# Reordering one-hots, gate copies and gate sums between the operand splits of a gate tile

## The chip, the cores and the metric

One core of one Trainium2 chip. The metric is the device time of one execution in microseconds; the kernel before took 3062.44 us (median of 3 runs, 3058.03 to 3063.49).

## The reference, cut to what matters

Two transformer blocks run over 256 tokens of width 2048 in float32. The first has an attention mixer and then a mixture over 16,384 tiny experts (`peer`); the second is another hybrid block. The change lies in `peer`:

```python
q = (xt @ wq).reshape(T, PEER_HEADS, 2, PEER_QDIM // 2)
...
idx = e1 * PEER_NKEYS + e2                  # 8 heads x 16 experts per token
gate = jax.nn.softmax(sc, axis=-1)
...
h = jax.nn.gelu(jnp.einsum('cd,chkd->chk', xc, u[ic]))
return jnp.einsum('chk,chkd->cd', gc * h, v[ic])
```

The kernel doesn't gather. It computes the hidden value of every expert for every token, builds a dense table of gates (zero where an expert wasn't chosen), multiplies the two and mixes all rows of `v`.

## The kernel before, in words

**Weights and splits.** All weights stream through two raw buffers of 1 MB (`raw`, 128 x 2048 floats); SyncE (SP) loads one such tile after another. A tile has two halves of 1024 columns. Each half is split into two reduced-precision parts that TensorE (PE) multiplies: ScalarE (ACT) writes `high` (`split_high`, L2270, the instruction is L2275), VectorE (DVE) writes `low = raw - high` (`split_low`, L1292, instruction L1296). There are four high and four low buffers. Half h uses buffer h % 4, and `split_high` waits until PE has used half h - 4 (`half_used`) and until the raw tile has landed. SP loads a raw buffer again when the low of its second half is written (`load`, L555). DVE and ACT work three halves ahead of PE (`LOOKAHEAD`).

**Experts, first pass.** 128 tiles of `u`, in 32 quads of four. For each tile, PE's `expert_hidden` (L1117) does, for either half, eight matmuls of 512 columns (high x both parts of the activations) and eight of 256 columns (low x high part). Every second tile, ACT copies the first results of a pair of tiles to SBUF (`first_hidden`, L2487, instruction L2493), DVE adds the second ones (`sum_hidden`, L1683, L1687), ACT applies gelu one tile later (`gelu`, L2496, L2499), and SP stores the pair, 256 KB, to `hidden_dram` (`store_hidden`, L574), in its queue between two loads.

**Gate tiles.** In quads 12 to 27 (16 quads, 64 tiles) each expert tile carries beside this the gates of four tokens. DVE's `onehots` (L1805) makes three tiles of 128x512: `first` (L1810), `second` (L1812), and `first_low` (L1815, `first` times the low part of the gate). ACT's `gate_first` (L2513, L2520) writes `first_high`, `first` times the high part of the gate, four instructions of 128x128. PE's `gates` (L1135) multiplies the one-hots of the four tokens after the tile's `expert_hidden`: four matmuls of 256 columns into two of the banks 4 to 7. There are two slots (`SLOTS`) for one-hots and for the result. Then ACT copies the high half of the result to `gates_out` (`copy_gates`, L2524, L2528) and DVE adds the low half (`sum_gates`, L1842, L1847). After each quarter (16 tiles, 64 tokens) ACT's queue issues eight stores of 512 KB to `gates_dram` (`store_gates`, L2547), one per tile in the first eight tiles of the next quarter; the last eight follow in the tiles behind the stage.

**The order of the work** is written out by hand for each engine; every engine takes its instructions in that order. In gate tile j of a quad both DVE and ACT split halves 2j + 3 and 2j + 4 and make the one-hots of tile j + 1:

- ACT: hidden step (`first_hidden` in even tiles, `gelu` in odd ones), two highs, `gate_first` of j + 1, `copy_gates` of j, and in some tiles a gate store.
- DVE: in even tiles `sum_hidden`, then two lows, `onehots` of j + 1, `sum_gates` of j.
- PE: `expert_hidden` of j (a wait for low in each half, one for the sum two tiles back), then `gates` of j, which waits for the sum of two tiles before (`gates_copied`), for the one-hots and for `first_high`.

Behind the stage come 16 expert tiles without gates, then the second pass over `v`.

Of the kernel before, what the change touches and what calls it, by code (L numbers as in the profile page):

```python
# [35 lines left out]
T = 256  # L36
# [7 lines left out]
LOOKAHEAD = 3  # L44
# [23 lines left out]
GATE_PIECES = 8  # L68
QUARTER = 64
# [14 lines left out]
CHOICE_QUADS = 12  # L84
PICK_ROWS = 4
GATE_QUADS = 16
# [21 lines left out]
def build(nc, ins, out):  # L108
    ctx = ExitStack()
    with ctx:  # L110
# [146 lines left out]
        def gate_parts(c):  # L257
            return bank[:, 4 + 2 * c:6 + 2 * c, :].rearrange("p b (u s e) -> p s e (b u)", s=2, e=P)
# [18 lines left out]
        dt_w = r4.take(KT * SSM_HEADS, "p (k n) -> p k n", k=KT)  # L277
        causal = r4.take(T)
        logits2, probs_t2, _, negmax2, expsum2 = attention_buffers(r4)
        dt_ = r4.take(4 * TT * SSM_HEADS, "p (k n) -> p k n", k=4)  # L280
        dt_tmp = r4.take(3 * TT * SSM_HEADS, "p (k n) -> p k n", k=3)
# [180 lines left out]
        def half(name, p, quad=0):  # L462


            q, p = quad + (quads[name] + p // QUAD), p % QUAD
            return p % SPLIT, p // 2 % RAW, p % 2, 2 * q + p // 4
# [58 lines left out]
        for n in range(UNITS):  # L525
            double, j, g = n // (2 * SET), n % (2 * SET) // 2, n % 2
# [4 lines left out]
                q=q1[part_of, c + (8 if swa else 0), :], k=k1[part_of, branch, :],  # L531
# [738 lines left out]
        def _(dve):  # L1270
# [21 lines left out]
            def split_low(h):  # L1292

                b, r, which, used = h
                dve.wait_ge(high_ready[b], used + 1)
                dve.tensor_tensor(low[b][:, :], raw[r][:, HALF * which:HALF * (which + 1)], as_f32(high[b][:, :]),  # L1296
                                  ALU.subtract).then_inc(low_ready[b], 1)
# [385 lines left out]
            def sum_hidden(n, j):  # L1683

                at = hidden[:, j % 2, :].rearrange("p (e t) -> p e t", e=2)
                dve.wait_ge(hidden_first, 2 * n + (j + 1))
                dve.tensor_tensor(at, at, bank[:, 2 * (j % 2):2 * (j % 2) + 2, T:], ALU.add).then_inc(hidden_summed, 1)  # L1687
# [111 lines left out]
            def split_tile_low(name, n, j):  # L1799
                if j % 2 == 0:  # L1800
                    sum_hidden(n, j // 2 - 1)
                split_low(half(name, 2 * j + LOOKAHEAD, n))
                split_low(half(name, 2 * j + LOOKAHEAD + 1, n))

            def onehots(n, j):  # L1805

                n, j = (n + 1, 0) if j == 4 else (n, j)
                c, token = j % SLOTS, 4 * FOUR * n + FOUR * j
                dve.wait_ge(gates_done[c], 2 * n + (j // 2 + PRIMED))
                dve.tensor_tensor(first[:, c, :, :], row(picked_t[:, 0, bass.ds(token, FOUR)], P), copies(iota[:, :], FOUR),  # L1810
                                  ALU.is_equal).then_inc(first_ready[c], 1)
                dve.tensor_tensor(second[:, c, :, :], row(picked_t[:, 1, bass.ds(token, FOUR)], P), copies(iota[:, :], FOUR),  # L1812
                                  ALU.is_equal)
                dve.wait_ge(first_ready[c], 2 * n + (j // 2 + 1))
                dve.tensor_tensor(first_low[:, c, :, :], first[:, c, :, :], row(picked_low[:, bass.ds(token, FOUR)], P), ALU.mult  # L1815
                                  ).then_inc(onehots_ready[c], 1)
# [25 lines left out]
            def sum_gates(q, n, j):  # L1842

                c = j % SLOTS
                at = gates_out[:, q % 2, :, bass.ds(4 * FOUR * n + (FOUR * j - QUARTER * q), FOUR)]
                dve.wait_ge(gates_first[c], 2 * n + (j // 2 + 1))
                dve.tensor_tensor(at, at, gate_parts(c)[:, 1], ALU.add).then_inc(gates_copied[c], 1)  # L1847

            def gate_tile(q, n, j, last=False):

                split_tile_low("experts_u_t", n + CHOICE_QUADS, j)
                if not last:
                    onehots(n, j + 1)
                sum_gates(q, n, j)

            onehots(0, 0)
            for q in range(T // QUARTER):
                with dve.Fori(GATE_QUADS // 4 * q, GATE_QUADS // 4 * (q + 1) - (q == T // QUARTER - 1)) as n:
                    for j in range(4):
                        gate_tile(q, n, j)  # L1860
            for j in range(4):
                gate_tile(T // QUARTER - 1, GATE_QUADS - 1, j, last=j == 3)
            with dve.Fori(0, EXPERT_QUADS - CHOICE_QUADS - GATE_QUADS - 1) as n:
                for j in range(4):
                    split_tile_low("experts_u_t", n + (CHOICE_QUADS + GATE_QUADS), j)
# [274 lines left out]
            for g in range(11):  # L2140
# [14 lines left out]
                for k in range(2):  # L2155
                    c, n = 4 * g + 2 * k, N * ((g - 3) % 2)
# [107 lines left out]
        def _(act):  # L2264
# [5 lines left out]
            def split_high(h):  # L2270

                b, r, which, used = h
                act.wait_ge(raw_landed[r], 16 * used + 16)
                act.wait_ge(half_used[b], used + PRIMED)
                act.activation(high[b][:, :], raw[r][:, HALF * which:HALF * (which + 1)], ACT.Copy  # L2275
                               ).then_inc(high_ready[b], 1)
# [210 lines left out]
            def first_hidden(n, j):  # L2487

                b, _, _, used = half("experts_u_t", 4 * j + 3, n)
                act.wait_ge(half_used[b], used + 1 + PRIMED)  # L2490
                if not (isinstance(n, int) and n == 0):
                    act.wait_ge(hidden_stored[j], 16 * n)
                act.activation(hidden[:, j, :].rearrange("p (e t) -> p e t", e=2), bank[:, 2 * j:2 * j + 2, 0:T],  # L2493
                               ACT.Copy).then_inc(hidden_first, 1)

            def gelu(n, j):  # L2496

                act.wait_ge(hidden_summed, 2 * n + (j + 1 + PRIMED))
                act.activation(hidden[:, j, :], hidden[:, j, :], ACT.Gelu_apprx_tanh).then_inc(gelu_done, 1)  # L2499

            def split_tile_high(name, n, j):
                split_high(half(name, 2 * j + LOOKAHEAD, n))
                split_high(half(name, 2 * j + LOOKAHEAD + 1, n))

            def hidden_tile(n, j):

                if j % 2 == 0:
                    first_hidden(n + (j // 2 - 1), 1 - j // 2)
                elif not (isinstance(n, int) and n == 0 and j == 1):
                    gelu(n + (j // 2 - 1), 1 - j // 2)  # L2510
                split_tile_high("experts_u_t", n, j)

            def gate_first(n, j):  # L2513

                n, j = (n + 1, 0) if j == 4 else (n, j)
                c = j % SLOTS
                act.wait_ge(first_ready[c], 2 * n + (j // 2 + 1))
                act.wait_ge(gates_done[c], 2 * n + (j // 2 + PRIMED))
                for t in range(FOUR):
                    m = act.activation(first_high[:, c, t, :], first[:, c, t, :], ACT.Copy,  # L2520
                                       scale=picked_t[:, 2, bass.ds(4 * FOUR * n + (FOUR * j + t), 1)])
                m.then_inc(first_high_ready[c], 1)

            def copy_gates(q, n, j):  # L2524

                c = j % SLOTS
                act.wait_ge(gates_done[c], 2 * n + (j // 2 + 1 + PRIMED))
                act.activation(gates_out[:, q % 2, :, bass.ds(4 * FOUR * n + (FOUR * j - QUARTER * q), FOUR)],  # L2528
                               gate_parts(c)[:, 0], ACT.Copy).then_inc(gates_first[c], 1)
# [22 lines left out]
                at = slice(piece * EXPERT_TILES // GATE_PIECES, (piece + 1) * EXPERT_TILES // GATE_PIECES)  # L2552
                act.dma_start(gates_dram[q, :, at, :], gates_out[:, q % 2, at, :]).then_inc(gates_stored[q % 2], 16)

            def gate_tiles(q, n, store=False, last=False):
                for j in range(4):
                    hidden_tile(n + CHOICE_QUADS, j)
                    if not (last and j == 3):
                        gate_first(n, j + 1)
                    copy_gates(q, n, j)  # L2560
                    if q and store:
                        store_gates(q - 1, 4 * (n - GATE_QUADS // 4 * q) + j)

            gate_first(0, 0)
            for q in range(T // QUARTER):
                if q >= 2:
                    act.wait_ge(gates_stored[q % 2], 16 * GATE_PIECES * (q // 2))
                for n in range(GATE_QUADS // 4 * q, GATE_QUADS // 4 * q + GATE_PIECES // 4):
                    gate_tiles(q, n, store=True)
                with act.Fori(GATE_QUADS // 4 * q + GATE_PIECES // 4, GATE_QUADS // 4 * (q + 1) - (q == T // QUARTER - 1)) as n:  # L2570
                    gate_tiles(q, n)
            gate_tiles(T // QUARTER - 1, GATE_QUADS - 1, last=True)
            for n in range(CHOICE_QUADS + GATE_QUADS, CHOICE_QUADS + GATE_QUADS + GATE_PIECES // 4):
                for j in range(4):
                    hidden_tile(n, j)
# [346 lines left out]
```

## Time and profile before

| | |
|---|---|
| median of 3 runs | 3062.44 us |
| the profiled execution | 3059.4 us, of which span 3057.6 |
| PE, DVE, ACT busy in the span | 3019.4, 2028.6, 1538.2 us |
| TensorE clock granted | 0.999 of full over the span |
| HBM traffic | 578.13 MB read, 36.49 MB written |

All durations below come from that one execution; times of day are microseconds from the start of its span. "Busy" counts the bars of an engine's instructions. Matmuls are pipelined and the end of a bar is modelled, so bars of neighbouring matmuls overlap. A merged row of the timeline (x8) gives the start of the first instruction and the time to the end of the last. `[0.67 <-ACT high L2275]` is idle time ahead of a row and what ended it.

### The profile page before, as it was taken

Reading aid. Unit: us, or ns where it says so; the run is one execution under the profiler, and the core shown is the slowest. Engines: PE = TensorE matmul, PEld = TensorE weight load, DVE = VectorE, ACT = ScalarE, POOL = GpSimd, SP = SyncE. Lnnn points to the kernel's source line nnn. Section 1 sums busy time; section 2 is a strip of 40 time slices with the busy share of each in tenths; the row PEclk is TensorE's granted clock in tenths of the full one; section 3 lists DMA queues with packets and bytes.
Section 4 is the critical chain, followed back from the end, with each engine's and each line's share of the span. In section 5 each row is a group of like instructions: output and inputs, shape, how many; then the busy total and the mean of one; then the engine's idle time right before and its main releaser. Section 6 shows DMA issues by size and latency. Waiting matters only on the chain.

```text
span 3057.6 us, 45171 instructions
## 1 busy us (share of the span) xinstructions
PE 3019.4 (99%) x16816; PEld 2615.9 (86%) x16816; DVE 2028.6 (66%) x2694; ACT 1538.2 (50%) x2134; POOL 20.6 (1%) x42
## 2 busy tenths in 40 slices
PE   9998999999999999999999999999999999999999
PEld 8997898888888888888888888888889888888887
DVE  5566679976888875555555555776566777777443
ACT  4554534555666665444444444544555555555333
POOL 2000000000000000000000000000000000000000
PEclk9999999999999999999999999999999999999999
DMA  7333545565566568766666666444455555555554
GB/s 269 133 132 116 188 159 196 204 228 187 186 239 240 213 219 296 249 240 242 242 241 241 241 241 233 163 147 163 152 179 179 181 195 187 191 180 192 196 189 179
DMA packets 138979, 615.20 MB, mean 201 GB/s; under 512 B 12989, under 2 KB 50062, under 8 KB 73968
## 3 DMA queue, kind: packets, MB, share of 16 engines
q1 hardware_dynamic: 126976, 583.05, 54.0%
q10 hardware_dynamic: 9440, 21.93, 2.0%
q0 software_dynamic: 2464, 8.89, 0.9%
q8 instruction: 63, 1.03, 0.1%
q14 instruction: 36, 0.29, 0.0%
HBM read 578.13 MB, written 36.49 MB: 201 GB/s over the span
## 4 chain that ended last, share of the span: by engine, by line
PE 76%; ACT 6%; DVE 5%; issue 3%; DMA 3%; ACTq 0%; DVEq 0%; SPq 0%
PE bank L642 75%; DMA raw<-in_experts_u_t 3%; ACT high L2275 3%; DVE low L1296 3%; ACT first_both L2520 1%; DVE first L1810 1%; ACT big L2528 1%; ACT big L2499 0%; ACT big L2493 0%; PE bank L912 0%; PE bank L732 0%; DMA raw<-in_w_down_t 0%; DVE resid L1928 0%; DVE big L1722 0%; ACT big L2307 0%
## 5 line engine op out<-in xcount | busy, mean ns | idle before, releaser
L1296 DVE TENSOR_TENSOR low<-raw,high 128x1024 fp32r<-128x1024 f32 x1008 | 1225.4, 1223 | 823.4 <-ACT high L2275 819.0
L2275 ACT ACTIVATE high<-raw 128x1024 fp32r<-128x1024 f32 x1008 | 1055.3, 1057 | 1064.9 <-PE bank L642 733.8
L642 PE MATMUL bank<-act_both,high 128*128 128x512 f32 (+1 forms) x5088 | 1169.2, 358 | 7.3 <-DVE low L1296 3.3
L642 PEld LDWEIGHTS bank<-act_both,high 128*128 128x128 f32 x5088 | 875.8, 190 | 123.5 <-issue 7.5
L642 PE MATMUL bank<-act_both,low 128*128 128x256 f32 x4240 | 713.3, 282 | 0.0
L642 PEld LDWEIGHTS bank<-act_both,low 128*128 128x128 f32 x4240 | 625.9, 191 | 33.1
L642 PE MATMUL bank<-high,weighed_high 128*128 128x512 f32 x1024 | 398.5, 389 | 0.0
L642 PE MATMUL bank<-high,weighed_low 128*128 128x512 f32 x1024 | 398.4, 389 | 0.0
L642 PE MATMUL bank<-low,weighed_high 128*128 128x512 f32 x1024 | 398.3, 389 | 0.0
L642 PE MATMUL bank<-high,act_both 128*128 128x512 f32 (+1 forms) x960 | 310.4, 393 | 3.6 <-DVE act_both L1358 3.6
L642 PEld LDWEIGHTS bank<-high,weighed_high 128*128 128x128 f32 x1024 | 192.3, 188 | 39.8
L642 PEld LDWEIGHTS bank<-low,weighed_high 128*128 128x128 f32 x1024 | 192.3, 188 | 39.8
L642 PEld LDWEIGHTS bank<-high,weighed_low 128*128 128x128 f32 x1024 | 192.3, 188 | 39.8
L642 PEld LDWEIGHTS bank<-high,act_both 128*128 128x128 f32 x960 | 180.7, 188 | 38.7 <-DVE act_both L1358 3.8
L642 PE MATMUL bank<-low,act_both 128*128 128x512 f32 (+1 forms) x480 | 185.8, 387 | 0.0
L2520 ACT ACTIVATE first_both<-first,taps 128x128 fp32r<-128x128 f32 x256 | 82.1, 391 | 129.2 <-DVE first L1810 129.2
L642 PE MATMUL bank<-high,ff_high 128*128 128x512 f32 x352 | 137.3, 390 | 0.4 <-DVE low L1296 0.4
L642 PE MATMUL bank<-low,ff_high 128*128 128x512 f32 x352 | 137.0, 389 | 0.0
L642 PE MATMUL bank<-high,ff_low 128*128 128x512 f32 x352 | 137.0, 389 | 0.0
L642 PE MATMUL bank<-big 128*128 128x64 f32 (+10 forms) x926 | 114.2, 303 | 6.5 <-DVE big L1635 2.3
L642 PEld LDWEIGHTS bank<-big 128*128 128x128 f32 (+5 forms) x926 | 95.2, 178 | 23.7 <-issue 7.3
L642 PEld LDWEIGHTS bank<-low,act_both 128*128 128x128 f32 x480 | 90.6, 189 | 16.9 <-issue 0.7
(286 smaller groups left out, 1923.1 us busy)
## 6 DMA issues: line engine op xcount, KB each, us to landing
raw<-in_experts_u_t SPq DMA_DIRECT2D x128, 1024.0 KB, 4.9
raw<-in_experts_v_t SPq DMA_DIRECT2D x128, 1024.0 KB, 4.8
raw<-in_w_up_t SPq DMA_DIRECT2D x88, 1024.0 KB, 4.8
raw<-in_w_in_t SPq DMA_DIRECT2D x68, 1024.0 KB, 4.8
raw<-in_w_down_t SPq DMA_DIRECT2D x44, 1024.0 KB, 4.8
raw<-in_w_out_t SPq DMA_DIRECT2D x32, 1024.0 KB, 4.8
raw<-in_peer_wq_t SPq DMA_DIRECT2D x16, 1024.0 KB, 4.8
hidden_dram<-big SPq DMA_DIRECT2D x64, 256.0 KB, 2.9
```

The source lines that it names most:

```text
L642: return pe.matmul(out_, lhs_t, rhs, start=start, stop=stop, skip_group_check=True)
L1296: dve.tensor_tensor(low[b][:, :], raw[r][:, HALF * which:HALF * (which + 1)], as_f32(high[b][:, :]), ALU.subtract).then_inc(low_ready[b], 1)
L1810: dve.tensor_tensor(first[:, c, :, :], row(picked_t[:, 0, bass.ds(token, FOUR)], P), copies(iota[:, :], FOUR), ALU.is_equal).then_inc(firs ...
L2275: act.activation(high[b][:, :], raw[r][:, HALF * which:HALF * (which + 1)], ACT.Copy).then_inc(high_ready[b], 1)
L2520: m = act.activation(first_high[:, c, t, :], first[:, c, t, :], ACT.Copy, scale=picked_t[:, 2, bass.ds(4 * FOUR * n + (FOUR * j + t), 1)])
L2528: act.activation(gates_out[:, q % 2, :, bass.ds(4 * FOUR * n + (FOUR * j - QUARTER * q), FOUR)], gate_parts(c)[:, 0], ACT.Copy).then_inc(g ...
```

## The change

On DVE, a gate tile's two lows are set apart: the first low comes first, then the hidden sum (even tiles), the gate sum of the tile before, the one-hots of the next tile, and then the second low. On ACT the first high comes first, then the hidden step, the gate copy of the tile before, the second high, and the scaling of the next one-hots (`gate_first`). The first tile of the stage has no copy and sum; those of the last tile follow behind it. For the first tile of each quarter, the copy and sum belong to the quarter before, so that DVE's first quad of a quarter is written out and its loops are one turn shorter. The instructions themselves and PE's and SP's programs are unchanged.

```diff
-            def gate_tile(q, n, j, last=False):
-
-                split_tile_low("experts_u_t", n + CHOICE_QUADS, j)
+            def gate_tile(q, n, j, sum_of=None, last=False):
+
+                split_low(half("experts_u_t", 2 * j + LOOKAHEAD, n + CHOICE_QUADS))
+                if j % 2 == 0:
+                    sum_hidden(n + CHOICE_QUADS, j // 2 - 1)
+                if sum_of is not None:
+                    sum_gates(sum_of, n, j - 1)
                 if not last:
                     onehots(n, j + 1)
-                sum_gates(q, n, j)
+                split_low(half("experts_u_t", 2 * j + LOOKAHEAD + 1, n + CHOICE_QUADS))
...
-                with dve.Fori(GATE_QUADS // 4 * q, GATE_QUADS // 4 * (q + 1) - (q == T // QUARTER - 1)) as n:
+                n0, last_q = GATE_QUADS // 4 * q, q == T // QUARTER - 1
+                for j in range(4):
+                    gate_tile(q, n0, j, q if j else (q - 1 if q else None))
+                with dve.Fori(n0 + 1, n0 + GATE_QUADS // 4 - last_q) as n:
                     for j in range(4):
-                        gate_tile(q, n, j)
+                        gate_tile(q, n, j, q)
...
+            sum_gates(T // QUARTER - 1, GATE_QUADS, -1)
...
-            def gate_tiles(q, n, store=False, last=False):
+            def gate_tiles(q, n, store=False, last=False, copy=True):
                 for j in range(4):
-                    hidden_tile(n + CHOICE_QUADS, j)
+                    split_high(half("experts_u_t", 2 * j + LOOKAHEAD, n + CHOICE_QUADS))
+                    if j % 2 == 0:
+                        first_hidden(n + (CHOICE_QUADS + j // 2 - 1), 1 - j // 2)
+                    else:
+                        gelu(n + (CHOICE_QUADS + j // 2 - 1), 1 - j // 2)
+                    if j or copy is not None:
+                        copy_gates(q if j else copy, n, j - 1)
+                    split_high(half("experts_u_t", 2 * j + LOOKAHEAD + 1, n + CHOICE_QUADS))
                     if not (last and j == 3):
                         gate_first(n, j + 1)
-                    copy_gates(q, n, j)
                     if q and store:
                         store_gates(q - 1, 4 * (n - GATE_QUADS // 4 * q) + j)
...
+            copy_gates(T // QUARTER - 1, GATE_QUADS, -1)
```

## Rows read from the trace of the kernel before

**Rows 1.** The page, part 1: busy time and share of each engine.

```profile
PE 3019.4 (99%) x16816; PEld 2615.9 (86%) x16816; DVE 2028.6 (66%) x2694; ACT 1538.2 (50%) x2134; POOL 20.6 (1%) x42
```

**Rows 2.** Windows: us, busy us and count per engine (PE, PEld, DVE, ACT, POOL), clock, DMA, GB/s.

```profile
737.80:804.50 66.70, 66.70 (x398) 59.33 (x397) 53.93 (x69) 43.99 (x85) 0.00 (x0) 1.00 0.52 187
804.50:1137.00 332.50, 327.38 (x1874) 284.07 (x1873) 269.60 (x338) 220.05 (x417) 0.00 (x0) 1.00 0.62 222
836.00:894.00 58.00, 56.97 (x326) 49.18 (x325) 47.31 (x59) 38.28 (x74) 0.00 (x0) 1.00 0.72 254
1137.00:1190.00 53.00, 52.83 (x300) 46.25 (x300) 28.56 (x28) 27.63 (x34) 0.53 (x1) 1.00 0.88 320
```

**Rows 3.** Timeline of PE: start, us, instruction; first, twelfth, last gates, and beyond.

```profile
737.82 0.64 PE L642 MATMUL bank<-first_both,second 128*128 128x256 f32 x4
...
801.76 2.00 PE L642 MATMUL bank<-act_both,high 128*128 128x512 f32 x8
803.60 1.11 PE L642 MATMUL bank<-act_both,low 128*128 128x256 f32 x8
804.55 0.64 PE L642 MATMUL bank<-first_both,second 128*128 128x256 f32 x4
...
1137.03 0.71 PE L642 MATMUL bank<-first_both,second 128*128 128x256 f32 x4
1137.62 2.10 PE L642 MATMUL bank<-act_both,high 128*128 128x512 f32 x8
...
1227.56 0.47 PE L642 MATMUL bank<-high,weighed_high 128*128 128x512 f32 x1
```

**Rows 4.** Timeline of PE, the end of a later tile.

```profile
918.48 1.11 PE L642 MATMUL bank<-act_both,low 128*128 128x256 f32 x8
919.64 0.71 PE L642 MATMUL bank<-first_both,second 128*128 128x256 f32 x4
```

**Rows 5.** Waits from 804.5 to 1137: who waited for whom, total us, times, longest.

```profile
ACT first_both L2520 <- DVE first L1810: 105.2, 52, 2.2
DVE big L1847 <- ACT big L2528: 40.4, 52, 1.0
```

**Rows 6.** Timeline of DVE, one tile and the start of the next.

```profile
908.75 2.37 DVE L1296 TENSOR_TENSOR low<-raw,high 128x1024 fp32r<-128x1024 f32 x2 [0.67 <-ACT high L2275]
911.03 0.69 DVE L1810 TENSOR_TENSOR first<-taps,iota 128x512 f32<-128x512 f32 x1
...
915.10 1.23 DVE L1296 TENSOR_TENSOR low<-raw,high 128x1024 fp32r<-128x1024 f32 x1
```

**Rows 7.** Timeline of ACT, the same tile.

```profile
911.87 1.28 ACT L2520 ACTIVATE first_both<-first,taps 128x128 fp32r<-128x128 f32 x4 [2.11 <-DVE first L1810]
913.06 0.57 ACT L2528 ACTIVATE big<-bank 128x512 f32 x1
913.53 0.58 ACT L2493 ACTIVATE big<-bank 128x512 f32<-128x512 f32 x1
914.01 2.16 ACT L2275 ACTIVATE high<-raw 128x1024 fp32r<-128x1024 f32 x2
```

**Rows 8.** DMA issues from 836 to 894: KB each, median us to landing.

```profile
raw<-in_experts_u_t SPq DMA_DIRECT2D x9, 1024.0 KB, 5.2
gates_dram<-big ACTq DMA_DIRECT2D x8, 512.0 KB, 4.7
```

**Rows 9.** Landing of the loads of L558, from 1137 to 1190.

```profile
DMA to landing us min/median/max: 4.9/5.7/7.4
```

**Rows 10.** Chain of waits from 883 to 897: start, us, what.

```profile
883.00 1.24 DVE low L1296
...
884.40 5.22 DMA raw<-in_experts_u_t
...
889.72 1.07 ACT high L2275
...
896.06 1.00 DVE low L1296
```

More of the change, by code:

```diff
@@ L1847, in sum_gates @@
                 dve.tensor_tensor(at, at, gate_parts(c)[:, 1], ALU.add).then_inc(gates_copied[c], 1)
-            def gate_tile(q, n, j, last=False):
-                split_tile_low("experts_u_t", n + CHOICE_QUADS, j)
+            def gate_tile(q, n, j, sum_of=None, last=False):
[4 more added lines that the diff above has]
+                    sum_gates(sum_of, n, j - 1)
                 if not last:
                     onehots(n, j + 1)
-                sum_gates(q, n, j)
+                split_low(half("experts_u_t", 2 * j + LOOKAHEAD + 1, n + CHOICE_QUADS))
             onehots(0, 0)
             for q in range(T // QUARTER):
-                with dve.Fori(GATE_QUADS // 4 * q, GATE_QUADS // 4 * (q + 1) - (q == T // QUARTER - 1)) as n:
+                n0, last_q = GATE_QUADS // 4 * q, q == T // QUARTER - 1
+                for j in range(4):
+                    gate_tile(q, n0, j, q if j else (q - 1 if q else None))
+                with dve.Fori(n0 + 1, n0 + GATE_QUADS // 4 - last_q) as n:
                     for j in range(4):
-                        gate_tile(q, n, j)
+                        gate_tile(q, n, j, q)
             for j in range(4):
-                gate_tile(T // QUARTER - 1, GATE_QUADS - 1, j, last=j == 3)
+                gate_tile(T // QUARTER - 1, GATE_QUADS - 1, j, T // QUARTER - 1, last=j == 3)
+            sum_gates(T // QUARTER - 1, GATE_QUADS, -1)
             with dve.Fori(0, EXPERT_QUADS - CHOICE_QUADS - GATE_QUADS - 1) as n:
@@ L2567, in _ @@
                     act.wait_ge(gates_stored[q % 2], 16 * GATE_PIECES * (q // 2))
[L2568 to L2572, printed above, removed]
+                n0 = GATE_QUADS // 4 * q
+                for n in range(n0, n0 + GATE_PIECES // 4):
+                    gate_tiles(q, n, store=True, copy=q if n > n0 else q - 1 if q else None)
+                with act.Fori(n0 + GATE_PIECES // 4, n0 + GATE_QUADS // 4 - (q == T // QUARTER - 1)) as n:
+                    gate_tiles(q, n, copy=q)
+            gate_tiles(T // QUARTER - 1, GATE_QUADS - 1, copy=T // QUARTER - 1, last=True)
+            copy_gates(T // QUARTER - 1, GATE_QUADS, -1)
             for n in range(CHOICE_QUADS + GATE_QUADS, CHOICE_QUADS + GATE_QUADS + GATE_PIECES // 4):
```

## Prediction

> **What bounds the kernel now.** TensorE counts as busy for 99% of the span [rows 1], so the first question is whether any other engine can hold it at all. In the stage that the change touches (64 gate tiles, about 733 to 1138 us) I split the stretch at the twelfth tile's gates and read the windows. Before and behind the split its matmul share looks alike: 66.70 of 66.70 us, then 327.38 of 332.50 us, both at a granted clock of 1.00, so the upper of the two levels, 2.4 GHz; clock is no part of this case [rows 2]. That view alone would put the recoverable time at 332.50 - 327.38 = 5.1 us. A matmul's bar, though, is longer than the distance to the next matmul, so bars cover short stalls.
>
> So I read starts. Each tile ends in four gate matmuls. The first such group starts at 737.82, the twelfth at 804.55, the sixty-fourth at 1137.03 [rows 3]. Eleven steps take 66.73 us, **6.066 us a tile**; the other 52 take 332.48 us, **6.394 us a tile**. The same instructions run on PE in both. 6.066 is what PE needs by itself: two halves of 2.79 us (801.76 to 804.55) and the rest, 0.48 us, of four gate matmuls. In a later tile the gates stand at 919.64 although the eight 256-column matmuls ahead of them began at 918.48; in an early tile such eight take 0.95 us (803.60 to 804.55), so PE stood there some 0.2 us [rows 3, 4]. Something paces PE, and only after twelve tiles, when the lead it had was used up.
>
> What paces it shows in the waits of that stretch: ACT waits 105.2 us in 52 tiles for the one-hot `first` of DVE, DVE waits 40.4 us in 52 for ACT's copy of the gates [rows 5]. Each waits for the other once per tile, in a ring. I followed one turn in the two timelines [rows 6, 7]: the pair of lows starts at 908.75, `first` at 911.03 (2.28), ACT's scaling at 911.87 (0.84), `copy_gates` at 913.06 (1.19), `first_hidden` at 913.53 (0.47), the next high at 914.01 (0.48), the next low at 915.10 (1.09). Sum 6.35 us, longer than PE's 6.07. So a ring of DVE and ACT bounds the tile, not either engine's load: DVE works 269.60 and ACT 220.05 of 332.50 us [rows 2].
>
> The Trainium skill ("Perfetto Trace Analysis", section "Identifying the Most-Contended Engine") says that matmul busy share is a poor measure of headroom and that the share of weight loads is a better one. The weight loads fall from 59.33/66.70 = 0.890 to 284.07/332.50 = 0.854 [rows 2]; at the early share the late loads would fit in 284.07/0.890 = 319.4 us, a gain of 13.1 us, against 5.1 by matmul bars and 17.05 by starts. I use the starts.
>
> **The change part by part.** No instruction is added or removed: per tile still two highs, two lows, three one-hot operations, four scalings, one gate copy, one gate sum, and per two tiles one first sum and one gelu. All that moves is their order on two queues.
>
> *DVE*: low1, hidden sum (every second tile), gate sum of the *last* tile, three one-hots, low2. *ACT*: high1, `first_hidden` or gelu, gate copy of the *last* tile, high2, four scalings.
>
> I check that PE's 6.07 can hold. Clock zero is the start of tile j-1's gate matmuls. Conservatively I use bar lengths, 0.69 us for a 128x512 operation of DVE, 0.58 and 0.57 for ACT's hidden step and copy, 1.28 for the four scalings, and 1.09 for a high [rows 6, 7]; a matmul's result counts 0.28 us behind its slot (the four gate matmuls show 0.64 and take 0.48, so 0.12 each, the last 0.28 long [rows 3]).
> - ACT: high1 needs the second half of tile j-1 used: 0.28 to 1.37. Hidden step to 1.95. Copy of tile j-1's gates (done by PE at 0.48 + 0.28 = 0.76, so no wait) to 2.52. high2 needs tile j's first half used, 0.48 + 2.79 + 0.28 = 3.55, to 4.64. Scalings need `first`.
> - DVE: low1 1.37 to 2.51 (2.28/2 = 1.14 each). Hidden sum to 3.20, gate sum to 3.89 (copy done at 2.52: this wait, 40.4 us before, goes), `first` 3.89, so ACT scales from 3.89 + 0.84 = 4.73 to 6.01. The other one-hots end at 5.96, low2 at 7.10.
> - The next turn begins with high1 at 6.35 and low1 at 7.44. ACT has 0.34 and DVE 0.34 us to spare in the heavier of two tiles; the scaled one-hots of tile j+1 are ready at 6.01 and PE wants them at 2 x 6.07 = 12.13.
>
> The rings left: low1, hidden sum, gate sum, `first`, scalings, next high1, next low1: 1.14 + 0.69 + 0.69 + 0.84 + 1.28 + 1.09 = 5.73 us, 5.04 without the hidden sum. Both below 6.07. What is late next is PE itself.
>
> *Waits that move.* In ACT's queue the copy now stands ahead of high2 and waits for PE's gates: 0.76 against its turn at 1.95, so nothing queues behind it; if that cover went, high2 and the scalings would follow it, and they have 6 us of lead over PE. high2 comes ahead of the scalings as before. The gate store of the last quarter now waits in the first tile of the next quarter for a sum made in that same tile: done at 3.89, asked for after the scalings, cost nothing, three times. gelu comes one high later, so SP's hidden store, which stands in SP's queue ahead of the next load, goes out some time after 1.95; the load behind it becomes free at low1's start + 1.40 (883.00 to 884.40 [rows 10]) = 2.77. It delays no load in the queue, but overlaps it more. POOL has nothing here. First and last tile keep their order apart from the swap.
>
> *The loads*, the one term that rows of before don't settle. A raw buffer is freed by low1 of tile j and wanted by high2 of tile j+1, then by high1 and low1 of tile j+2. Before, in a tile pair with gate stores, that ring took 883.00 to 896.06 = 13.06 us with a landing of 5.22 [rows 10], so 7.84 us beside the load, 6.53 a tile. After, beside the load: 1.40 to issue, 0.1 from landing to high2 (889.62 to 889.72), high2 1.09, scalings 1.28, high1 to low1 1.09, together 4.96. At 5.2 (median in store tiles, [rows 8]) the pair takes 10.2, below 12.13; the load binds from a landing of 7.2. The slowest landing behind the stage, where the same stores and the loads make 320 GB/s, is 7.4 [rows 2, 9]; that in all 24 store tiles would cost 24 x ((4.96 + 7.4)/2 - 6.07) = 2.7 us. The best end is no cost. I take 0, since the store tiles' own median is nearer: they carry 254 GB/s now, at 6.07 some 270, still below 320.
>
> The Trainium skill ("DMA: Bandwidth & Descriptors", section "Issuing engines are not separate DMA queues") says that transfers issued by different engines interleave on the same 16 DMA engines. By it the later hidden store and the gate stores take time from the load, which is the first rival below; by the rows the sum has 0 for it.
>
> **Sum**: 52 x (6.394 - 6.066) = 17.05 us. Behind the stage PE runs at its own pace but for 0.7 us (1137.62 to 1227.56 is 89.94, 32 halves of 2.79 are 89.28 [rows 3]), which I leave out of the sum. The profiled execution took 3059.4 us (its span 3057.6 and 1.8 around it): 3042.4 after. It lies 3.0 below the median of the runs, 3062.44: **3045.4**.
>
> **The rivals.**
> 1. *The loads keep the store tiles where they are.* 24 of the 64 tiles carry a 512 KB store beside the load [rows 8], and the hidden store comes closer. If they stay at 6.53, 24 x 0.46 = 11.1 us of the 17.05 are not won: 3056.5. For it: those are the slowest tiles now. Against: most of their ring was not the load (7.84 of 13.06). Chance 0.09.
> 2. *Given back or moved*: the lead that PE wins is lost in the 16 tiles behind the stage, or another wait of the same size takes the ring's place: no change, 3062. Against: PE can't bank work there, two raw buffers hold it, and that stretch ran at PE's pace when entered without lead. Chance 0.05.
> 3. *Slower*: with gelu's store issued just ahead of the load and ACT's gate store beside it, landings in the store tiles double to 10.4. Then a tile takes (4.96 + 10.4)/2 = 7.68, 24 x 1.15 = 27.6 us more than today, less the 5.95 won elsewhere: +21.7, 3084. It decides from a landing of 9.1 (7.03 a tile). Nothing in the trace landed that late. Chance 0.05.
> 4. The order doesn't do what it says, or a short wait that I don't see costs part: 3050 to 3055. Chance 0.05.
>
> **How the numbers follow.** The forecast has 0.76. A measurement of this kernel tells about 0.2% from no change, 6.1 us. Faster: 0.76 + 0.05 + half of rival 1 = 0.85; same 0.10; slower 0.05. Range: 3041 (the lowest run of before, 3058.03, less 17.05) to 3057 (rival 1).
>
> **What would show it.** Right: gate groups 6.07 us apart through all 64 tiles with bars of 0.64; the 105.2 us of ACT waiting for `first` nearly gone and ACT's highs waiting for PE instead; the gate sum waiting for nothing; loads in store tiles below 7.2. Wrong: store tiles still near 6.5, ACT's high2 waiting for its load, or gate groups even but the 16 tiles behind longer than 89.9.

## The result, and the profile after

The changed kernel takes 3044.37 us (median of 6 runs, 3041.6 to 3045.7) against 3061.81 us for the kernel before in the same session (6 runs, 3058.03 to 3063.49). The ratio is 0.9944 [0.9931, 0.9957], a gain of 17.4 us. The forecast was 3045.4 us from a gain of 17.05.

The profiled execution of after took 3045.70 us, with a span of 3043.9. The page hardly shows what happened: the busy time of each engine, part 1, is within 0.5% of what it was [rows 1].

```profile
PE 3012.0 (99%) x16816; PEld 2617.3 (86%) x16816; DVE 2021.5 (66%) x2694; ACT 1541.1 (51%) x2134; POOL 20.5 (1%) x42
```

The chain that ended last, part 4 of the page, does show it. The first fence is before, the second after (shares of the span; "issue" is time without a visible wait, a name with q is an engine's sequencer).

```profile
PE 76%; ACT 6%; DVE 5%; issue 3%; DMA 3%; ACTq 0%; DVEq 0%; SPq 0%
```

```profile
PE 91%; DVE 2%; ACT 1%; issue 1%; DMA 0%; DVEq 0%; ACTq 0%; SPq 0%
```

ACT, DVE and DMA had 14% of the chain between them and now have 3%; PE has the rest. Where the time went is read from starts of gate groups, as in [rows 3]. The timeline of PE after has the first, second, twelfth and sixty-fourth group of the stage, and the first matmul of the pass over `v`:

```profile
741.87 0.64 PE L642 MATMUL bank<-first_both,second 128*128 128x256 f32 x4
747.94 0.64 PE L642 MATMUL bank<-first_both,second 128*128 128x256 f32 x4
...
808.61 0.64 PE L642 MATMUL bank<-first_both,second 128*128 128x256 f32 x4
...
1124.07 0.64 PE L642 MATMUL bank<-first_both,second 128*128 128x256 f32 x4
...
1213.96 0.47 PE L642 MATMUL bank<-high,weighed_high 128*128 128x512 f32 x1
```

The 63 steps take 1124.07 - 741.87 = 382.20 us, **6.067 a tile from the first to the last**; before they took 399.21. That is 17.01 us. Between the two profiled executions the span differs by 13.7: the unchanged part ahead of the stage was 4.05 us longer in this one, the stage 17.01 shorter, the rest 0.74 shorter. This execution is the slowest of the six, so the median gains more than it does.

Windows of after, the 52 tiles behind the twelfth and a stretch of tiles with stores, beside [rows 2] (columns as there):

```profile
808.60:1124.10 315.50, 315.50 (x1875) 280.64 (x1874) 262.14 (x336) 221.20 (x412) 0.00 (x0) 1.00 0.68 235
840.00:895.00 55.00, 55.00 (x328) 48.88 (x327) 45.58 (x59) 38.55 (x74) 0.00 (x0) 1.00 0.80 270
```

PE's bars leave no gap in the 52 tiles, and the store tiles carry the 270 GB/s that the prediction had estimated. The weight loads fill 280.64 / 315.50 = 0.890 of them, the share of the first twelve tiles before. The Trainium skill ("Perfetto Trace Analysis", section "Identifying the Most-Contended Engine") names that share as a better measure of headroom than matmul bars. In this trace it came closer than the bars, 13.1 us against 5.1, but only the starts gave the 17.0 that is measured.

Waits of after from 808.6 to 1124 (who waited for whom, total us, times, longest):

```profile
ACT high L2283 <- PE bank L642: 73.7, 87, 1.5
DVE low L1296 <- ACT high L2283: 53.1, 57, 1.4
ACT high L2283 <- DMA raw<-in_experts_u_t: 19.4, 10, 2.5
```

Both waits of [rows 5] are gone. ACT now waits for PE, that is, for buffers that PE still uses, and DVE for ACT behind it: the followers wait for the engine that sets the pace. The waits for loads have grown: 19.4 us in 10, where the kernel before had this, from 804.5 to 1137:

```profile
ACT high L2275 <- DMA raw<-in_experts_u_t: 6.8, 17, 0.8
```

They come back below.

One tile of DVE and of ACT after, beside [rows 6, 7]:

```profile
894.90 1.23 DVE L1296 TENSOR_TENSOR low<-raw,high 128x1024 fp32r<-128x1024 f32 x1 [0.75 <-ACT high L2283]
896.04 0.68 DVE L1687 TENSOR_TENSOR big<-big,bank 128x512 f32<-128x512 f32 x1
896.64 0.68 DVE L1847 TENSOR_TENSOR big<-big,bank 128x512 f32 x1
897.24 0.69 DVE L1810 TENSOR_TENSOR first<-taps,iota 128x512 f32<-128x512 f32 x1
...
900.96 1.23 DVE L1296 TENSOR_TENSOR low<-raw,high 128x1024 fp32r<-128x1024 f32 x1 [0.70 <-ACT high L2283]
...
906.97 1.23 DVE L1296 TENSOR_TENSOR low<-raw,high 128x1024 fp32r<-128x1024 f32 x1 [1.23 <-ACT high L2283]
```

```profile
893.80 1.06 ACT L2283 ACTIVATE high<-raw 128x1024 fp32r<-128x1024 f32 x1 [0.57 <-PE bank L642]
894.77 0.58 ACT L2501 ACTIVATE big<-bank 128x512 f32<-128x512 f32 x1
895.25 0.59 ACT L2536 ACTIVATE big<-bank 128x512 f32 x1
897.01 1.06 ACT L2283 ACTIVATE high<-raw 128x1024 fp32r<-128x1024 f32 x1 [1.18 <-PE bank L642]
898.06 1.28 ACT L2528 ACTIVATE first_both<-first,taps 128x128 fp32r<-128x128 f32 x4
```

DVE runs hidden sum, gate sum and `first` without idle time ahead of any (L1687, L1847, L1810 have no bracket) and then waits 0.70 to 1.23 us per tile for the next high. ACT makes `first_both` at 898.06, 0.82 us behind the start of `first`, without waiting.

### The profile page after: what moved, and what is told of

Same layout as the page of the kernel before. It is cut to its first block, busy times and chain, and to the rows that moved or that the text cites. A ratio compares the mean times of both kernels' runs of the same rounds, so it can differ in the third digit from the quotient of the medians.

```text
span 3043.9 us, 45078 instructions
## 1 busy us (share of the span) xinstructions
PE 3012.0 (99%) x16816; PEld 2617.3 (86%) x16816; DVE 2021.5 (66%) x2694; ACT 1541.1 (51%) x2134; POOL 20.5 (1%) x42
## 4 chain that ended last, share of the span: by engine, by line
PE 91%; DVE 2%; ACT 1%; issue 1%; DMA 0%; DVEq 0%; ACTq 0%; SPq 0%
PE bank L642 90%; DVE low L1296 1%; ACT high L2283 1%; PE bank L912 0%; PE bank L732 0%; DMA raw<-in_w_down_t 0%; DVE resid L1936 0%; DVE big L1722 0%; PE bank L808 0%; DVE big L1635 0%; ACT act_both L2368 0%; ACT big L2315 0%; DVE big L1696 0%; DVE big L1700 0%; DVE act_both L1358 0%
## 5 line engine op out<-in xcount | busy, mean ns | idle before, releaser
L642 PEld LDWEIGHTS bank<-act_both,low 128*128 128x128 f32 x4240 | 627.0, 191 | 33.1
L2218 DVE SCALAR_TENSOR_TENSOR taps<-bank,conv,taps 128x255 f32<-128x255 f32 (+1 forms) x176 | 72.7, 475 | 25.7 <-ACT taps L2761 25.7
```

What stands on the lines that cost most here:

```text
L642: return pe.matmul(out_, lhs_t, rhs, start=start, stop=stop, skip_group_check=True)
L2218: m = dve.scalar_tensor_tensor(taps[:, j, q, tap:T], plain, w[:, 4 * q + 2 - tap:4 * q + 3 - tap], taps[:, j, q, tap:T], ALU.mult, ALU.add)
```

## The experiments

Each change is told by its diff; ratios are to runs of the kernel before on the same chip in the same session.

### DVE's order alone

The DVE part of the diff ahead of the prediction, with ACT as before (copy of the same tile's gates last, scaling of the one-hots ahead of it).

> VectorE in the new order, ScalarE in the old one. Ring theory (the time of a tile is the longest closed chain of waits between DVE and ACT, counted by the spacings in the trace of before): low1 1.14, hidden sum 0.60 (even tiles), gate sum 0.60 (its copy is long done), first to scaling 0.84, scalings 1.19, copy 0.47, hidden step 0.48, high1 to low1 1.09: 6.41 us in even, 5.81 in odd tiles, 6.11 on average, against PE's 6.067. That is so close that the lead covers it: gate groups 6.07 to 6.11 apart, 0 to 3 us slower than the changed kernel, ratio to before 0.9945 to 0.9955. Rival (both halves of the change are needed, each wait gives its own share): the wait of DVE for the copy, 40 us before, goes, the wait of ACT for the one-hots, 105 us, stays; about half the gain, ratio 0.997 to 0.998.

Measured: 3045.63 us, ratio 0.9943 [0.9926, 0.9959]. The gate groups run from 741.57 to 1123.77, the same 382.20 us. Timeline of DVE, the first lows of three tiles (what stands between them left out):

```profile
987.96 1.22 DVE L1296 TENSOR_TENSOR low<-raw,high 128x1024 fp32r<-128x1024 f32 x1 [1.08 <-ACT high L2283]
...
993.74 1.23 DVE L1296 TENSOR_TENSOR low<-raw,high 128x1024 fp32r<-128x1024 f32 x1 [1.02 <-ACT high L2283]
...
1000.16 1.23 DVE L1296 TENSOR_TENSOR low<-raw,high 128x1024 fp32r<-128x1024 f32 x1 [1.06 <-ACT high L2283]
```

The turns take 5.78 and 6.42 us, on average 6.10, so here the ring of DVE and ACT is level with PE's 6.07. In the waits from 740 to 1120 ACT still stands for the one-hots:

```profile
ACT first_both L2528 <- DVE first L1810: 79.0, 61, 1.8
```

So 79 us of a named wait cost nothing: a wait is lost time only if the ring that it closes is longer than PE's tile. The kernel before shows the same: ACT waited for `first` 22.1 us in its first eleven tiles, while PE ran at 6.07, and 105.2 in the later 52, the same 2.0 us a tile.

### ACT's order alone

The ACT part alone, DVE as before.

> ScalarE in the new order, VectorE in the old one. Ring theory: from high1 0.97, hidden step 0.50, copy to gate sum 0.72, gate sum 0.60, hidden sum 0.60 (even tiles), two lows 2.28, first to scaling 0.84, scalings 1.19, next high1: 7.7 us in even, 7.1 in odd tiles, 7.4 on average. So it is slower than before: 64 x (7.4 - 6.24) = 74 us less what the lead still covers, some 5: 3125 to 3140 us, ratio 1.02 to 1.026; gate groups 7.2 to 7.5 apart once the lead is gone. Rival (each half of the change gives a share of the gain by itself): not slower than before, ratio 0.995 to 1.000.

Measured: 3115.89 us, ratio 1.0177 [1.016, 1.0194], slower by 54.8 us. Waits from 740 to 1190, and three gate groups of PE:

```profile
ACT first_both L2520 <- DVE first L1810: 176.6, 62, 3.5
DVE big L1847 <- ACT big L2528: 137.8, 62, 2.6
...
PE bank L642 <- DVE low L1296: 32.0, 54, 0.9
...
PE bank L642 <- ACT first_both L2520: 5.4, 27, 0.5
```

```profile
909.16 0.71 PE L642 MATMUL bank<-first_both,second 128*128 128x256 f32 x4 [0.27 <-ACT first_both L2520]
...
916.78 0.71 PE L642 MATMUL bank<-first_both,second 128*128 128x256 f32 x4 [0.18 <-ACT first_both L2520]
...
923.85 0.71 PE L642 MATMUL bank<-first_both,second 128*128 128x256 f32 x4 [0.18 <-ACT first_both L2520]
```

The groups stand 7.62 and 7.07 us apart (7.52 and 6.97 in about half of the tiles). PE now waits visibly, mostly for lows, 32.0 us, and a little for the scaled one-hots, 5.4. Both waits of [rows 5] have grown: DVE sums a tile's gates ahead of its next low, and ACT copies them only after its next high and hidden step. The same two engines, the same instructions and a busy share no higher: what decides is where the chain closes. The total lies 9 us below the lower end of what was expected. The 63 steps took 455.32 us, 56 more than before, where 69 had been worked out: the last 60 steps took 7.29 on average instead of 7.4, which is 7 us, and the expectation set them against 6.24 us a tile, where the kernel before needs 399.21 / 63 = 6.34, which is 6 more.

### The one-hots between the lows, and nothing else

The kernel before with one edit on DVE. The gate copy and sum stay with their own tile, ACT is untouched.

```diff
-                split_tile_low("experts_u_t", n + CHOICE_QUADS, j)
+                if j % 2 == 0:
+                    sum_hidden(n + CHOICE_QUADS, j // 2 - 1)
+                split_low(half("experts_u_t", 2 * j + LOOKAHEAD, n + CHOICE_QUADS))
                 if not last:
                     onehots(n, j + 1)
+                split_low(half("experts_u_t", 2 * j + LOOKAHEAD + 1, n + CHOICE_QUADS))
                 sum_gates(q, n, j)
```

> The kernel before with one edit: VectorE makes the next one-hots between its two lows; hidden sum first, gate sum of the same tile last, as before; ScalarE unchanged. Ring theory: low1 1.14, first to scaling 0.84, scalings 1.19, copy 0.47, hidden step 0.48, high1 to low1 1.09: 5.2 us, below 6.067, and DVE's own work, 5.0 on average, too. PE paces every tile: gate groups 6.07 apart, the whole gain, ratio 0.9935 to 0.995; in tiles with gate stores the load's ring is 5.7 + landing per two tiles, which at 6.5 is 12.2 against 12.13, covered by the lead. Rival (the delayed copy and sum are what lets the engines run apart, since they wait for PE's gates of the same tile): gate groups at 6.2 to 6.4, ratio 0.997 to 1.000.

Measured: 3041.51 us, ratio 0.9933 [0.9917, 0.995]. Timeline of PE, first and last gate group:

```profile
737.62 0.64 PE L642 MATMUL bank<-first_both,second 128*128 128x256 f32 x4
...
1119.83 0.64 PE L642 MATMUL bank<-first_both,second 128*128 128x256 f32 x4
```

382.21 us. Its waits from 740 to 1119:

```profile
DVE big L1847 <- ACT big L2531: 33.1, 61, 0.7
...
ACT first_both L2523 <- DVE first L1810: 6.9, 24, 0.7
```

One moved group of instructions gives the whole gain. DVE still waits 33.1 us for the gate copy (47.8 over the stage before), and PE loses nothing by it; what cost was the ring that ran through both lows to `first`.

### The changed kernel again, beside these

> The changed kernel beside the others on one chip. Both theories: ratio 0.993 to 0.9955, gate groups 6.07 apart.

Measured: 3043.6 us, ratio 0.994 [0.9923, 0.9956]. The two microseconds by which the one-edit kernel was ahead were followed up with five more runs of each, on another chip:

> The one edit again (one-hots between the lows, all else as before), with more rounds. Ring theory: the same time as the changed kernel within 2 us, since PE paces all 64 tiles in both and nothing else differs; ratio 0.993 to 0.995. Rival (its shorter landings leave something behind the stage): 3 us or more faster than the changed kernel.

> The changed kernel beside it, same chip and rounds: ratio 0.993 to 0.9955.

Measured: 3044.17 us, ratio 0.995 [0.9936, 0.9963], for the one-edit kernel, 3042.09 us, ratio 0.9945 [0.9931, 0.9958], for the changed one. The order turned round, so the two are equal as far as these runs tell. None of these versions beats the changed kernel.

### How much DVE can bear

To the changed kernel's one-hots comes a sum that nothing uses, over 512 columns, or 1536, once a tile. The lead in the expectations is the time by which DVE and ACT are ahead of PE.

```diff
+                dve.wait_ge(more_done, 4 * n + (j + PRIMED))
+                dve.tensor_reduce(picked_place[:, 1, 1, 0:2], resid[:, 0, 0:512].rearrange("p (a n) -> p a n", a=2), AX.X, ALU.add
+                                  ).then_inc(more_done, 1)
```

> The changed kernel with one more instruction of VectorE in every gate tile, a sum over 512 columns that nobody uses, some 0.6 us, behind the second one-hot. Ring theory: in the changed kernel DVE idles 0.7 us ahead of low1 in even and 1.2 us in odd tiles; 0.6 fits, gate groups stay 6.07 apart, ratio as the changed kernel, 0.9925 to 0.9960. Rival (there is no spare, DVE's time in a gate tile is on the path): 64 x 0.6 = 38 us more, ratio 1.004 to 1.008.

> The same with a sum over 1536 columns, some 1.7 us. Ring theory: DVE's own row of a tile becomes the longest ring: even 1.14 + 0.6 + 0.6 + 1.8 + 1.7 + 1.14 = 7.0 us, odd 6.4, 6.68 on average, 0.61 above PE's 6.067. PE goes on at 6.07 until its lead of some 6 us is used, about ten tiles, and then at 6.6 to 6.7: 64 x 0.61 - 6 = 33 us above the changed kernel, 3070 to 3082, ratio 1.003 to 1.007. Rival (DVE's time is on the path from the first tile): gate groups above 6.6 from the start and 64 x 1.7 = 109 us, ratio above 1.02.

Measured with 512 columns: 3043.66 us, ratio 0.995 [0.9934, 0.9967], groups at 6.07; with 1536: 3075.94 us, ratio 1.0055 [1.0039, 1.0072]. Windows from 741 to 838 of the first and of the second kernel:

```profile
741.00:838.00 97.00, 97.00 (x578) 86.28 (x577) 91.91 (x124) 69.66 (x132) 0.00 (x0) 1.00 0.57 203
```

```profile
741.00:838.00 97.00, 94.71 (x539) 81.34 (x538) 97.00 (x110) 62.42 (x117) 0.00 (x0) 1.00 0.50 182
```

At 91.91 of 97.00 busy DVE costs nothing; at 97.00 of 97.00 it is the bound, and the 63 steps grow by 33.2 us to 415.40. PE in the second kernel:

```profile
902.09 0.71 PE L643 MATMUL bank<-first_both,second 128*128 128x256 f32 x4
903.18 2.08 PE L643 MATMUL bank<-act_both,high 128*128 128x512 f32 x8 [0.38 <-DVE low L1297]
...
908.85 0.64 PE L643 MATMUL bank<-first_both,second 128*128 128x256 f32 x4
...
915.36 0.71 PE L643 MATMUL bank<-first_both,second 128*128 128x256 f32 x4
```

The groups are 6.76 and 6.51 us apart, and PE waits for a low, not for one-hots. The total was as expected; the place was not: only the first four steps ran at 6.07, where about ten had been expected. From 741 to 1154 PE waited 11.0 us for lows and never visibly for one-hots, so it is the lows that come too late first, and they have less lead.

### What slow loads do

To each of the 64 tiles comes one more store of 512 KB in ACT's queue, of data that nothing uses: once in the changed kernel, once in the one-edit kernel above.

```diff
+                    act.dma_start(extra_dram[bass.ds(4 * n + j, 1)].rearrange("a p n -> p (a n)"), resid[:, 0, 0:HALF]).then_inc(extra_stored, 16)
```

> The changed kernel with one more 512 KB store of ScalarE's queue in each of the 64 gate tiles (from the residual to a scratch tensor), so 1.7 MB per tile everywhere and 2.2 MB in the 24 store tiles. The load's ring by the prediction: 4.96 us + landing per two tiles, against 12.13. In tiles with one store landings are 6.0 to 6.5 now, so those hold 6.07; in tiles with two stores 2.2 MB in 6.07 us would be 367 GB/s, more than the 320 seen, so landings of 8 to 9 and 6.5 to 7 us a tile, of which the lead takes 6 us in each run of eight: 0 to 8 us above the changed kernel, ratio 0.993 to 0.998. Rival (loads bind as soon as they land later than 7.2, or the extra stores delay ACT): the store tiles at 7 or more and over 20 us above the changed kernel, ratio above 1.001.

> The same extra stores in the kernel before with the one-hots between the lows (the one edit alone). Its load's ring is longer, 5.7 us + landing per two tiles, since the copy and the hidden step stand in it; it binds from a landing of 6.4 instead of 7.2. If landings grow as in the changed kernel, it is the slower of the two, by 24 x 0.37 = up to 9 us. Rival (its landings stay short, as in its run without extra stores, where they were 4.9 in store tiles against 6.0 in the changed kernel, because its hidden and gate stores go out farther from the load): as fast as the changed kernel with extra stores or faster.

Measured: the changed kernel with these stores 3045.77 us, ratio 0.9956 [0.9941, 0.997]; the one-edit kernel with them 3076.41 us, ratio 1.0046 [1.0028, 1.0063]. A landing is the time from a load's issue to its arrival. Landings of the loads over the stage, the first over 741 to 1124, the second over 741 to 1154:

```profile
DMA to landing us min/median/max: 5.0/7.5/9.3
```

```profile
DMA to landing us min/median/max: 5.0/7.6/9.9
```

Nearly the same landings, and times 30.6 us apart. In the changed kernel ACT waits 100.4 us for loads, and PE lost only 384.30 - 382.20 = 2.1 us, all of it late, most of it in one step of 6.37 and in the last one:

```profile
1124.31 0.71 PE L644 MATMUL bank<-first_both,second 128*128 128x256 f32 x4 [1.56 <-ACT first_both L2530]
```

The ring of a raw buffer shows in SP's timeline: a load's issue to the next issue into the same buffer, less the landing in between. First the changed kernel, with a landing of 8.0 for the load at 924.77, then the one-edit kernel, with 6.0 for the load at 917.35 (x2 is a merged row, the second load goes to the other buffer):

```profile
924.77 6.95 SPq L560 DMA_DIRECT2D raw<-in_experts_u_t  x2
...
937.67 5.66 SPq L560 DMA_DIRECT2D raw<-in_experts_u_t  x2
```

```profile
917.35 5.72 SPq L560 DMA_DIRECT2D raw<-in_experts_u_t  x2
...
929.03 0.33 SPq L560 DMA_DIRECT2D raw<-in_experts_u_t  x1
```

12.90 - 8.0 = 4.90 us beside the load in the changed kernel, where 4.96 had been worked out; 11.68 - 6.0 = 5.68 in the other; 7.84 before [rows 10]. With landings of 7.5 the one makes (4.9 + 7.5) / 2 = 6.2 us a tile, so little over PE's 6.07 that the lead covers most of it. With 7.6 the other makes 6.64, and by this estimate 64 x 0.57 less 6 us of lead, 30 us, are lost. Its 63 steps took 411.13 us, 28.9 more than PE's 382.20: fourteen ran at 6.07, the others at 6.66 on average. So of the 30.6 us between the two kernels 26.8 lie in the stage. The one-edit kernel had been expected to lose 9 us at most, for the landings were priced in 24 store tiles alone; here they are slow from the first tile on (median 7.6 from 741 to 836, 5.7 in the changed kernel). Why the same store slows them sooner there wasn't tried, so the 26.8 us are not the longer ring's alone.

### The hidden step ahead of the first high

Loads in the store tiles land later after the change (6.5 us in the median from 838 to 893, 5.2 before). Two causes are possible: SP's hidden store, which now goes out closer to the load, or ACT's gate store beside it. The changed kernel with the hidden step moved back ahead of the first high parts them:

```diff
-                    split_high(half("experts_u_t", 2 * j + LOOKAHEAD, n + CHOICE_QUADS))
                     if j % 2 == 0:
                         first_hidden(n + (CHOICE_QUADS + j // 2 - 1), 1 - j // 2)
                     else:
                         gelu(n + (CHOICE_QUADS + j // 2 - 1), 1 - j // 2)
+                    split_high(half("experts_u_t", 2 * j + LOOKAHEAD, n + CHOICE_QUADS))
```

> The changed kernel with ScalarE's hidden step (first_hidden or gelu) ahead of the first high again; all else as changed. In the changed kernel loads in tiles with gate stores land in 6.0 to 6.5 us, in the kernel with the one edit in 4.9. Theory A: the cause is the hidden store, which goes out 0.6 us ahead of the load instead of 2.1; with gelu a high earlier it goes out about 1.6 us ahead, landings of 5.0 to 5.6. Theory B: the cause is the gate store, 1.1 us behind the load instead of 2.6; it stays where it is, and so do the landings, 6.0 and more. By both PE still paces the tiles: gate groups 6.07 apart, ratio 0.992 to 0.996.

Measured: 3042.98 us, ratio 0.9945 [0.993, 0.9961]. Timeline of SP in a store tile, first the changed kernel, then this one:

```profile
853.20 0.35 SPq L577 DMA_DIRECT2D hidden_dram<-big  x1
853.83 0.33 SPq L558 DMA_DIRECT2D raw<-in_experts_u_t  x1
```

```profile
849.46 0.36 SPq L577 DMA_DIRECT2D hidden_dram<-big  x1
851.56 0.33 SPq L558 DMA_DIRECT2D raw<-in_experts_u_t  x1
```

Landings of the loads from 838 to 893, in the same order:

```profile
DMA to landing us min/median/max: 4.8/6.5/8.0
```

```profile
DMA to landing us min/median/max: 4.8/5.3/6.0
```

With 2.10 us between the 256 KB store and the load, as before the change (856.43 and 858.53), the median landing is back at 5.3; with 0.63 us it is 6.5. The gate store stands 1.07 us behind the load in the one and 1.06 in the other, so its place isn't what differs. How the hidden store does it is not shown in full: only every second load has it right ahead, and in the changed kernel the others, at 847.78, 859.9 and 872.0, land late too, in 6.5, 6.8 and 8.0 us, against 5.1 to 5.3 here. The time doesn't change, since by these medians neither ring reaches 6.07.

## Why the prediction was right, and where its steps were not

**The bound, and the size of the gain: right.** A ring of DVE and ACT, not the load of either, held 52 tiles at 6.394, and PE's own 6.066 took its place: 52 x 0.328 = 17.05 forecast, 17.01 in the traces, 17.4 by the medians. The first and third experiment show the ring as the cause: with `first` taken out from behind the second low, the tile falls to 6.07 whatever else stays. The second shows the arithmetic of rings: turns worked out at 7.1 and 7.7 us, 7.07 and 7.62 measured in the steps shown, 6.97 and 7.52 in others.

**Which part of the change earns it: not asked.** The sum gave the gain to the change as a whole and listed the wait for the gate copy, 40.4 us, beside that for `first`. The runs part them: moving the one-hots earns everything, moving the copy and the hidden step nothing in this kernel's own conditions. What they bring is a shorter ring of the raw buffers, 4.9 against 5.7 us beside the load, which pays only when loads land late; with the extra stores the changed kernel was 30.6 us ahead, in part because its loads were slowed later.

**The loads: the term of 0 held, the reason did not.** The landing cost was set to 0 because the store tiles' own median of 5.2 was nearer than 7.4, and the loads were to stay below 7.2. They rose: 4.8/6.5/8.0 from 838 to 893, 4.8/6.3/8.3 in the next store tiles. The median stayed below the binding 7.2, some loads did not, and the ten waits of 19.4 us for loads all fall in these tiles. PE lost nothing by them: the sum gave this no place, but DVE and ACT have a lead over PE, some 6 us by the prediction's clock (one-hots ready at 6.01, wanted at 12.13), and single late loads can be paid from it. That the term came out at 0 is in part luck. The prediction had named the mechanism, the later hidden store that "overlaps it more", and then given it nothing. The last experiment bears it out, 6.5 against 5.3 us in the median, though SP issues both this store and the load. The Trainium skill ("DMA: Bandwidth & Descriptors", section "Issuing engines are not separate DMA queues") says that transfers from different issuers interleave on the same DMA engines; the run with ACT's extra stores agrees, for SP's loads land in 7.5 us in the median of the stage there, and in 5.0 without these stores. So the condition of the first rival came true in part, and its price did not follow.

**The spare time: too small.** From bar lengths DVE had 0.34 us to spare in the heavier tile. Its timeline shows 0.70 and 1.23: an instruction of 0.69 us lets the next one start after 0.60. For a bound on the safe side bars are right, for a budget they are not; the sum over 512 columns fitted in.

**The other rivals.** Nothing was given back: 1124.55 to 1213.96 behind the stage is 89.41 us, 89.94 before. No landing in the stage doubled: the longest took 8.3. (The third rival's "nothing in the trace landed that late" misses the second load of the whole program, which took 10.8 in the kernel before; from 20 us on the longest took 7.9.) Of the 0.7 us that the prediction left out behind the stage 0.5 were won.

**The signs.** Even groups with bars of 0.64, the wait of 105.2 us gone, ACT's highs waiting for PE and the gate sum for nothing: all there. That no load in a store tile lands after 7.2 us: wrong.

## What to carry to other kernels

When two in-order engines wait for each other once per tile, follow one turn from start to start until it closes, and compare it with the tile of the engine that ought to be the bound; their busy shares (66% and 50% before) and the sums of their waits say little, and one group of instructions moved out of the ring can be the whole gain. Price a repeated stage by the distance between the starts of a matmul group that occurs once per tile, not by the gaps between bars. If an edit moves the issue of a store, look at how far it then stands from the next load, and at the lead over the bound engine from which a late load can be paid.

## What was not expected of the hardware

- Loads of 1 MB landed later when a store of 256 KB ahead of every second one stood closer, those in between included: with 2.1 to 2.2 us between the two, loads from 838 to 893 land in 5.3 us in the median and 6.0 at most, with 0.6 to 1.0 us in 6.5, and single ones in 8.0.
- The transfers moved 341 GB/s in the changed kernel with the extra stores, more than the 320 of [rows 2], and PE's bars filled the window still. The window of that kernel from 838 to 895:

```profile
838.00:895.00 57.00, 57.00 (x340) 50.69 (x339) 45.85 (x59) 38.61 (x74) 0.00 (x0) 1.00 0.94 341
```
